# A transformer-layer kernel with its opening rewritten: gain row by TensorE, late constants, one weight group for two token tiles, zero matmuls

## What is computed

```
def _rms_norm(x, gain):
    xf = x.astype(jnp.float32)
    y = xf * lax.rsqrt(jnp.mean(xf * xf, axis=-1, keepdims=True) + RMS_EPS)
    return (y * gain.astype(jnp.float32)).astype(x.dtype)

def _swiglu(x, w_in, w_out):
    g, u = jnp.split(x @ w_in, 2, axis=-1)
    return (jax.nn.silu(g) * u) @ w_out
...
        h = _swiglu(_rms_norm(x, ffn1_pre_norm[l]), ffn1_w_in[l], ffn1_w_out[l])
```

## Time and profile before

| quantity | value |
|---|---|
| median of 3 runs | 942.28 us (941.71 to 942.32) |
| span of the profiled execution | 940.6 us, some 1.7 us less than the median |
| PE busy | 910.5 us, 97% of the span |
| DVE, ACT, POOL busy | 563.0 (60%), 451.7 (48%), 80.4 us (9%) |
| DMA | 169.18 MB, mean 180 GB/s, 345 GB/s in the first fortieth of the span |

### The profile page before, as it was taken

One profiled execution on the slowest core, in us unless ns is written; L12 is line 12 of the kernel. 1 busy time (PEld: TensorE's weight loads), 2 busy tenths in 40 slices (PEclk: granted clock), 3 DMA queues, 4 the chain that ended last, 5 costly groups with the idle time before them and its releaser, 6 DMA issues.

```text
span 940.6 us, 11364 instructions
## 1 busy us (share of the span) xinstructions
PE 910.5 (97%) x4160; PEld 748.2 (80%) x4160; DVE 563.0 (60%) x625; ACT 451.7 (48%) x541; POOL 80.4 (9%) x107
## 2 busy tenths in 40 slices
PE   4999999999999999999999999999999799999997
PEld 3888888878888888888788888887887578888885
DVE  4755444466766556567655553555949866666653
ACT  5644444354533445436544443344877354444441
POOL 3000000003232200000000000000361200000000
PEclk9999999999999999999999999999999899999999
DMA  9744553637644443444544453755433454444421
GB/s 345 245 185 194 194 197 140 250 130 257 214 171 163 169 154 138 154 159 179 223 179 178 178 186 134 300 202 182 170 123 117 152 192 182 185 178 178 178 90 45
DMA packets 25684, 169.18 MB, mean 180 GB/s; under 512 B 3392, under 2 KB 3568, under 8 KB 6448
## 3 DMA queue, kind: packets, MB, share of 16 engines
q1 hardware_dynamic: 22752, 159.92, 45.7%
q0 software_dynamic: 2752, 8.69, 2.8%
q10 hardware_dynamic: 144, 0.07, 0.0%
HBM read 167.61 MB, written 1.05 MB: 179 GB/s over the span
## 4 chain that ended last, share of the span: by engine, by line
PE 89%; DVE 4%; ACT 3%; issue 2%; DMA 1%; SPq 0%; DVEq 0%; ACTq 0%
PE acc L1305 27%; PE acc L1307 26%; PE acc L1306 26%; DMA raw<-weights 1%; DVE w_lo L810 1%; PE aux L1425 1%; PE aux L1606 1%; PE aux L1358 1%; ACT w_hi L430 1%; PE aux L1306 1%; PE aux L1305 1%; PE aux L1307 1%; PE aux L1468 1%; PE aux L1518 1%; PE aux L1485 1%
## 5 line engine op out<-in xcount | busy, mean ns | idle before, releaser
L810 DVE TENSOR_TENSOR w_lo<-raw,w_hi 128x2048 fp32r<-128x2048 f32 x147 | 334.9, 2302 | 150.4 <-ACT w_hi L430 116.0
L1305 PE MATMUL acc<-w_hi,xT_hi 128*128 128x512 f32 x880 | 351.6, 400 | 6.0 <-DVE w_lo L810 3.0
L1307 PE MATMUL acc<-w_hi,xT_lo 128*128 128x512 f32 x880 | 344.7, 392 | 0.0
L1306 PE MATMUL acc<-w_lo,xT_hi 128*128 128x512 f32 x880 | 343.8, 391 | 0.0
L430 ACT ACTIVATE w_hi<-raw 128x2048 fp32r<-128x2048 f32 x97 | 184.0, 1912 | 91.1 <-PE acc L1307 75.9
L1305 PEld LDWEIGHTS acc<-w_hi,xT_hi 128*128 128x128 f32 x880 | 165.9, 188 | 41.3 <-DVE w_lo L810 4.7
L1307 PEld LDWEIGHTS acc<-w_hi,xT_lo 128*128 128x128 f32 x880 | 165.7, 188 | 35.8
L1306 PEld LDWEIGHTS acc<-w_lo,xT_hi 128*128 128x128 f32 x880 | 166.1, 189 | 32.8
L444 ACT ACTIVATE w_hi<-raw 128x2048 fp32r<-128x2048 f32 x52 | 96.6, 1910 | 0.9 <-issue 0.9
L532 ACT ACTIVATE silu_g<-acc 128x256 f32<-128x256 f32 x44 | 16.9, 383 | 121.5 <-PE acc L1307 121.5
L1305 PE MATMUL acc<-w_hi,hT_hi 128*128 128x512 f32 x176 | 69.8, 396 | 0.0
(11 more groups left out here) (176 smaller groups left out, 774.2 us busy)
## 6 DMA issues: line engine op xcount, KB each, us to landing
raw<-weights SPq DMA_DIRECT2D x149, 1024.0 KB, 4.9
gain_pre<-gains POOLq DMA_DIRECT2D x5, 512.0 KB, 6.8
bias_raw<-bias_in POOLq DMA_DIRECT2D x32, 64.0 KB, 2.3
gain_post<-gains POOLq DMA_DIRECT2D x3, 512.0 KB, 6.1
gate_w<-gate_w_in POOLq DMA_DIRECT2D x1, 1536.0 KB, 7.0
x<-x_in SPq DMA_DIRECT2D x2, 512.0 KB, 8.0
raw<-weights SPq DMA_DIRECT2D x2, 512.0 KB, 7.8
out<-tmp SPq DMA_DIRECT2D x4, 256.0 KB, 2.1
```

Of the source, the lines that this page charges most:

```text
L810: v.tensor_tensor(w_lo[:, slot], raw[:, slot], w_hi[:, slot].bitcast(F32), ALU.subtract)\
L1305: m.matmul(dst, hi[:, k, cols], w_hi[:, slot, w], start=first, stop=False)
L1306: m.matmul(dst, hi[:, k, cols], w_lo[:, slot, w], start=False, stop=False)
L1307: return m.matmul(dst, lo[:, k, cols], w_hi[:, slot, w], start=False, stop=last)
```

## The change

Four things are done to the opening; the rest of the program is the same.

1. The broadcast of the first gain row leaves SP's queue. ACT's queue loads the row as it is (4 KB, `gain_row`) ahead of `ident`, and PE multiplies a row of ones with it: two matmuls of K = 1 and 512 columns in plain float32, into `acc[:, 1, 1]` and `acc[:, 1, 0]`. DVE waits for both (`gain0_spread`) and reads the gains from there.
2. SP issues x of tile 1 ahead of weight group 1. ACT does the squares of tile 1 ahead of the rounding of group 1, and DVE the norm of tile 1 ahead of its `w_lo`. ACT rounds the first half of group 0 ahead of the two `xT_hi` copies. POOL's constants wait until group 1 has landed.
3. PE uses group 0 for both token tiles (`half_tile`), and then group 1 for both.
4. PE does three zero matmuls of 128x256 in plain float32 (`keep_warm`) before the gain matmuls, and three more after the transposes of tile 0. DVE sets their operands (`warm`, `ones_row`) by two memsets at the start.

The diff, cut to its core:

```diff
         @block.sync
         def _(sp):
             sp.dma_start(x[:, 0, :], x_in[0:P, :]).then_inc(x_landed[0], 16)
-            sp.dma_start(gain_pre[:], gains[0:1, :].partition_broadcast(P)).then_inc(gain0_landed, 16)
...
-                if g == 1:
+                if g == 0:
                     sp.dma_start(x[:, 1, :], x_in[P:2 * P, :]).then_inc(x_landed[1], 16)
...
+            pool.wait_ge(landed[1], 16)
             for dst, src in ((colmask, colmask_in), (conv_a, conv_a_in), (conv_ab, conv_ab_in),
...
                     second(0)
-                    parts(0)
                     act.wait_ge(half_landed, 16)
                     a.activation(w_hi[:, 0, 0:GROUP // 2], raw[:, 0, 0:GROUP // 2], ACT.Copy).then_inc(half_hi, 1)
+                    parts(0)
                     act.wait_ge(landed[0], 16)
                     a.activation(w_hi[:, 0, GROUP // 2:], raw[:, 0, GROUP // 2:], ACT.Copy).then_inc(hi_done, 1)
                     split[0] = 1
-                    round_to(2)
                     second(1)
                     parts(1)
                     round_to(4)
...
+            act.dma_start(gain_row[:], gains[0:1, :]).then_inc(gain0_landed, 16)
             act.dma_start(ident[:], ident_in).then_inc(ident_landed, 16)
...
-                        dve.wait_ge(gain0_landed, 16)
+                        dve.wait_ge(gain0_spread, 2)
...
+                        gain = gain_pre[:, part] if n else acc[:, 1, 1 if h == 0 else 0]
                         v.scalar_tensor_tensor(tmp[:, t, part], x[:, t, part], rstd[:, 2 + t:3 + t],
-                                               gain_pre[:, part], ALU.mult, ALU.mult).then_inc(xn_ready, 1)
+                                               gain, ALU.mult, ALU.mult).then_inc(xn_ready, 1)
...
                         low_half(0, 0)
                         low_half(0, 1)
-                        low_to(2)
...
+            v.memset(ones_row[:], 1.0).then_inc(warm_set, 1)
+            v.memset(warm[:], 0.0).then_inc(warm_set, 1)
             norm(*NORMS[0])
...
+            def half_tile(g, par, t, half):
+
+                if t == 0:
+                    if g == 0 and half == 0:
+                        pe.wait_ge(half_lo, 1)
+                    else:
+                        pe.wait_ge(lo_done, g + half + 1)
+                for unit in range(4):
+                    if g == 0 and half == 0 and t == 0 and unit == 2:
+                        pe.wait_ge(lo_done, 1)
+                    i = product(acc[:, t, par], xT_hi, xT_lo, 4 * half + unit, t, (g + half) % RING, unit,
+                                half == 0 and unit == 0, half == 1 and unit == 3)
...
+            def keep_warm(times):
+
+                for _ in range(times):
+                    m.matmul(acc[:, 0, 0, 0:256], warm[:, 0:P], warm[:, P:P + 256], start=True, stop=True)
...
                 if n == 0:
+                    pe.wait_ge(warm_set, 2)
+                    keep_warm(3)
+                    pe.wait_ge(gain0_landed, 16)
+                    for h in range(2):
+                        m.matmul(acc[:, 1, 1 - h], ones_row[:], gain_row[:, h * 512:(h + 1) * 512],
+                                 start=True, stop=True).then_inc(gain0_spread, 1)
                     run(0)
+                    keep_warm(3)
+                    wait_operand(1)
+                    half_tile(0, 0, 0, 0)
+                    run(1)
+                    wait_operand(3)
+                    half_tile(0, 0, 1, 0)
+                    wait_operand(4)
+                    for t in range(T):
+                        half_tile(0, 0, t, 1)
+                    for t in range(T):
+                        column_tile(2, (2) % RING, 1, t)
+                    return
```

More of the change, by code:

```diff
@@ L167, in build @@
         prod = at("prod", [P, 2, T, 256], F32, area + 47104)
+        warm = at("warm", [P, P + 256], F32, area + 47104)
+        ones_row = at("ones_row", [1, P], F32, area + 49152)
+        gain_row = at("gain_row", [1, DM], F32, area + 53248)
         nqT = [at(f"nqT{i}", [P, NH // 2, S], F32, area + 4096 * i) for i in range(2)]
@@ L229, in build @@
         gain0_landed = sem("gain0_landed")
+        warm_set = sem("warm_set")
+        gain0_spread = sem("gain0_spread")
         gains_in = sem("gains_in")
@@ L1307, in product @@
                 return m.matmul(dst, lo[:, k, cols], w_hi[:, slot, w], start=False, stop=last)
+            def half_tile(g, par, t, half):
[9 more added lines that the diff above has]
+                                half == 0 and unit == 0, half == 1 and unit == 3)
+                if half:
+                    i.then_inc(acc_full[t], 1)
+                elif t == 1:
+                    i.then_inc(group_used, 1)
+            def keep_warm(times):
+                for _ in range(times):
+                    m.matmul(acc[:, 0, 0, 0:256], warm[:, 0:P], warm[:, P:P + 256], start=True, stop=True)
             def column_tile(g, slot0, par, t, before_half=None):
@@ L1313, in column_tile @@
                         before_half(half)
[L1314 to L1317, removed]
+                    if t == 0:
                         pe.wait_ge(lo_done, g + (half + 1))
                     for unit in range(4):
-                        if by_halves and unit == 2:
-                            pe.wait_ge(lo_done, 1)
                         i = product(acc[:, t, par], xT_hi, xT_lo, 4 * half + unit, t, (slot0 + half) % RING, unit,
@@ L1390, in first_columns @@
                 if n == 0:
-                    run(0)
-                wait_acc_free(pe, 0, FIRST_ACC[st])
[L1394 to L1405, removed]
+                    pe.wait_ge(warm_set, 2)
[4 more added lines that the diff above has]
+                                 start=True, stop=True).then_inc(gain0_spread, 1)
+                    run(0)
+                    keep_warm(3)
[10 more added lines that the diff above has]
+                    return
+                wait_acc_free(pe, 0, FIRST_ACC[st])
+                column_tile(g0, g0 % RING, 0, 0, operand(0))
                 column_tile(g0 + 2, (g0 + 2) % RING, 1, 0, lambda half: run(1) if half else None)
```

## The result

| | before | after |
|---|---|---|
| median | 942.3 us (941.71 to 943.31, 4 runs) | 948.4 us (948.11 to 948.87, 4 runs) |
| ratio | | 1.006, 95% interval 1.0048 to 1.0072 |
| span of the profiled execution | 940.6 us | 946.3 us |
| start of the 25th product | 23.33 | 29.06 |
| span less that start | 917.3 | 917.2 |

The changed kernel is slower by 6.1 us; +1.2 had been forecast, with a range that ended at +4.0. The last two lines of the table say where the time went: all 5.7 us of the span are lost ahead of the 25th product, and the stretch behind it is as long as before.

What follows compares the result with a forecast made beforehand. PE, busy for 97% of the span, was taken as the bound, so only the opening could shift: 5.2 (`ident`) + 5.5 (gain work) + 13.8 (to the 25th product) - 23.33 = +1.2, 943.5 us; range 940.9 to 946.3.

Steps and rivals of the forecast that it cites:

- the sign: Whole kernel: slower, by +1.2 us to 943.5 us; slower by over 0.2% had chance 0.30.
- `ident` at 5.2: PE's start: the identity lands at 4.76 + 0.41 = 5.2, one issue later for the gain row ahead of it.
- The gain work: PE's opening after `ident`: three zero and two gain matmuls, from 5.2 to 10.7.
- G: Moment both gain matmuls are done and DVE can start; forecast at 10.7, against a first normalization at 6.94 before.
- the clock rises somewhere inside this: Zero and gain matmuls: PE's clock goes high 4.5 us after its start, at 9.7, giving G = 10.7.
- The all-low bound: Zero and gain matmuls all at the low clock: 5.2 + 2.6 + 3.4 + 0.2, so G = 11.4.
- G + 13.8: Start of the 25th product, when group 1's `w_lo` is done, with PE at the high clock after G.
- G + 5.05: First product: PE may start at the first half `w_lo` of group 0, 5.05 us after G.
- the low-clock rival: Clock still low at the first product: G = 11.4, +2.75 to +5.2 us, middle +3.9, 946.2 us; chance 0.20.
- the untouched wait for `ident`: PE's start: the wait stays ahead of the zero matmuls, making early memsets useless; PE starts at 5.2.
- mark: Start of the 25th product, 23.33 before; if PE never waits after it, the span changes by its shift.
- the cost of a float32 matmul from the earlier trace: Zero and gain matmuls: two instructions each; per 256-column instruction 0.216 us high, 0.43 low, twice that for 512 columns.

Runs made afterwards that it cites:

- the probe: The changed kernel with eight more K = 1 matmuls of the first gain half ahead of the two that count; span 961.0 us in one run.

## Why the prediction was wrong

The path was right (DVE waits for the gain matmuls, these for the identity) and the sign too; three terms of the sum were too small. It read +1.2 = 5.2 + 5.5 + 13.8 - 23.33. The trace reads 7.63 + 6.67 + 14.76 - 23.33 = +5.73.

- **`ident` at 5.2 (measured 7.63, +2.4).** The step "the row of gains is now issued ahead of it on ACT's queue, which takes one issue, 0.41" failed. I priced the moved load at its issue and left out what the queue does behind it. The identity lands 6.3 us after its own issue in place of 4.0 (5.6 to 6.5 in the five kernels with the row ahead of it); with the order swapped it is 4.0 again. One row of 4 KB was not worth half a microsecond but 2.9 (7.63 less the 4.75 of the swapped order).
- **The gain work, 5.5 us from PE's start to G (measured 6.67, +1.2).** The step "the clock rises somewhere inside this" failed. It had the rise 4.5 us after PE's start. That much holds for the zeros with the transposes behind them: in the kernel with the gain by DMA they start at 4.78, and the next three zeros, at 9.29, take 1.46, the high rate. With the gain matmuls in between, the same zeros at 17.06, 9.4 us after PE's start, still take 2.77, and in the probe twenty K = 1 instructions stay low for 17.4 us. So the forecast wrongly took the gain matmuls to be as good for the clock as other work. Which property of them it is (one row, the columns, the data) stays open. The all-low bound (5.2 + 6.2 = 11.4) was the right branch; its parts, 2.6 and 3.4, measured 2.85 and 3.82 with first and last instruction.
- **G + 13.8 (measured G + 14.76, +1.0).** It assumed the high clock. The transposes ran low (1.97 us for eight), so the second copy of ACT came 0.7 late, and the first product came at G + 5.6 and not G + 5.05; the second three zeros at the low rate (2.77) ended at 19.83, when `w_lo` was just there. That is part of what I had set down for the low-clock rival. The rise came with the first products: twelve of them took 3.16 us (19.91 to 23.07) in place of 2.8, and not the 5.3 of that rival.

That the sign came out is worth little, since a slowing of over 0.2% had been given only a chance of 0.30. What was right: DVE's first step now released by the gain matmuls; the untouched wait for `ident` that makes the early memsets useless (moving it is worth 6.3 us of mark); the cost of a float32 matmul from the earlier trace rows; PE's two waits of 1.0 us before the 25th product, and none behind it; and that the constants and group 2 cost nothing after it. The forecast and the low-clock rival were two cases of one sum, and the true time lay above both since the identity was off in either. Its landing had no bound from above; one more landing of 4.0 us, 8.8, would have been an honest one.

What the Trainium skill (TensorE: Matmul & The Clock Gate, Part 4: PE-mode transpose) says of transposes, that they don't count as busy in the way matmuls do, was not settled. In two kernels transposes are PE's only work ahead of the first product: the kernel before (1.94 us, then 2.98 us of waiting) and the one with neither gain matmuls nor zeros (1.94 us, then 2.64). The products behind them start low in both. That agrees with the page, but the waiting may be the reason as well. In the changed kernel the level was low before any transpose: the gain matmuls themselves ran at the low rate, 3.78 us for four instructions.

So the change failed by one of its four parts. Reorder, shared group, late constants and zeros together won 2.3 us once the gain row was left to DMA. Their worth can't be added up: with the zeros out the mark is at 23.95, with the group not shared at 26.34, both behind the 23.33 of the kernel before, and with the constants early at 22.99. And the new order has a fault of its own: the rounding of group 1 behind the copies of tile 1 costs 0.9 us of mark (21.01 less 20.10).

## What to carry to other kernels

Before an engine is given a job at the start of a program, list what it waits for there: a wait that used to be hidden (the identity matrix, needed 3 us later) becomes the start of everything. A small load put ahead of a needed one on the same queue can delay its landing by far more than its issue: 2.9 us here, for 4 KB. Spreading a row by TensorE in plain float32 is dear: 3.8 us for 1024 columns at the low level, and two instructions 0.863 us apart for 512 columns where one product of 512 columns takes 0.43. In these runs it brought nothing for the clock either. Filler matmuls of zeros on 128 rows did, and they are worth having only where PE would idle.

## What the runs showed of the hardware

- Twenty K = 1 float32 matmul instructions of 512 columns in a row kept the low level for 17.4 us; during 38 zero instructions on 128 rows, 7.5 to 18.2, it rose to the high one.
- Behind 1.98 us of K = 1 instructions and the transposes of one tile, the level fell from high to low although PE had been busy for 3.1 of the last 4.1 us. With the constants early it fell behind 1.32 us of transposes and 1.4 us of waiting around them.
- A 4 KB load of one partition ahead of a 64 KB load on ACT's queue: 6.3, 5.7, 5.6, 6.5 and 6.1 us from issue to landing for the latter in five kernels, 4.0 without it.
- Behind the transposes of tile 1 and a wait of 4.86 us the level was low, and twelve products took 5.3 us in place of 2.8.
